# Two stage barriers of a one-core transformer trunk removed, its semaphores recycled, routing tables and gate products moved into the last output tiles

## What is computed

```python
x = x + m_lat[2] * y                                   # y: token mixer's output @ w_out
h = modulate(rmsnorm(x, norm2_w), m_lat[3], m_lat[4])
aff = softmax(h @ router_w)                            # 2048 tokens x 16 experts
gate, idx = lax.top_k(swapaxes(aff, 1, 2), 256)        # each expert takes its 256 best tokens
xs = h[idx]
hid = silu(xs @ w1[e]) * (xs @ w3[e])
y = (hid @ w2[e]) * gate
x = x + m_lat[5] * scatter_add(y, idx)
out = rmsnorm(x, final_norm_w)
```

## Time and profile before

| | us |
|---|---|
| median of 3 runs (lowest, highest) | 2226.61 (2224.59, 2227.75) |
| the profiled execution | 2225.62 |
| its span, first to last instruction | 2223.9 |
| busy: PE, DVE, ACT, POOL | 2118.4 (95%), 1372.4 (62%), 993.1 (45%), 282.8 (13%) |

### The profile page before, as it was taken

One profiled execution on the slowest core, in us unless ns is written; L12 is line 12 of the kernel. 1 busy time (PEld: TensorE's weight loads), 2 busy tenths in 40 slices (PEclk: granted clock), 3 DMA queues, 4 the chain that ended last, 5 costly groups with the idle time before them and its releaser, 6 DMA issues. The chain is left out here.

```text
span 2223.9 us, 34721 instructions
## 1 busy us (share of the span) xinstructions
PE 2118.4 (95%) x13389; PEld 1847.9 (83%) x13389; DVE 1372.4 (62%) x2077; ACT 993.1 (45%) x1619; POOL 282.8 (13%) x356
## 2 busy tenths in 40 slices
PE   6999999999999799995799999999999999999995
PEld 4778888777777588883799999999999999999993
DVE  3663648995974666746455655556555565555656
ACT  5822544344622444421444444444444444444444
POOL 0000000000001001011111122111221112211120
PEclk9999999999999899996799999999999999999997
DMA  7473333343337656328347656476565765657655
GB/s 253 147 262 105 112 92 96 122 123 94 101 121 218 230 173 199 124 108 306 129 182 254 207 199 213 180 258 207 196 213 180 261 207 190 216 180 264 207 182 225
DMA packets 188283, 407.92 MB, mean 183 GB/s; under 512 B 15956, under 2 KB 53396, under 8 KB 187300
## 3 DMA queue, kind: packets, MB, share of 16 engines
q1 hardware_dynamic: 162068, 317.84, 41.1%
q0 software_dynamic: 26128, 88.92, 12.6%
HBM read 329.59 MB, written 77.12 MB: 183 GB/s over the span
## 5 line engine op out<-in xcount | busy, mean ns | idle before, releaser
L55 PE MATMUL bh<-xt_hi,shi 128*128 128x256 f32 x2048 | 580.8, 284 | 3.2 <-DVE slo L2234 3.2
L56 PE MATMUL bh<-xt_lo,shi 128*128 128x256 f32 x2048 | 580.7, 284 | 0.0
L57 PE MATMUL bh<-xt_hi,slo 128*128 128x256 f32 x2048 | 580.6, 284 | 0.0
L2234 DVE TENSOR_TENSOR slo<-raw,shi 128x1024 fp32r<-128x1024 f32 x384 | 455.9, 1222 | 162.3 <-ACT shi L2152 157.8
L2152 ACT ACTIVATE shi<-raw 128x1024 fp32r<-128x1024 f32 x384 | 388.8, 1050 | 127.3 <-PE eby L57 127.3
L55 PEld LDWEIGHTS bh<-xt_hi,shi 128*128 128x128 f32 x2048 | 393.9, 192 | 4.3 <-issue 3.7
L56 PEld LDWEIGHTS bh<-xt_lo,shi 128*128 128x128 f32 x2048 | 393.9, 192 | 0.6
L57 PEld LDWEIGHTS bh<-xt_hi,slo 128*128 128x128 f32 x2048 | 393.8, 192 | 0.0
L55 PE MATMUL bank<-h_hi,whi 128*128 128x512 f32 x704 | 286.3, 407 | 0.0
L56 PE MATMUL bank<-h_lo,whi 128*128 128x512 f32 x704 | 278.7, 396 | 0.0
L57 PE MATMUL bank<-h_hi,wlo 128*128 128x512 f32 x704 | 278.3, 395 | 0.0
(11 more groups left out here) (336 smaller groups left out, 3145.4 us busy)
## 6 DMA issues: line engine op xcount, KB each, us to landing
raw<-in_exp_w_dram SPq DMA_DIRECT2D x96, 2048.0 KB, 11.1
uT<-stage POOLq DMA_DIRECT2D x72, 256.0 KB, 2.7
xb<-in_ada_w_dram SPq DMA_DIRECT2D x24, 512.0 KB, 5.6
wraw<-in_w_in_dram SPq DMA_DIRECT2D x22, 512.0 KB, 5.1
adaw<-in_ada_w_dram SPq DMA_DIRECT2D x8, 1024.0 KB, 10.0
xb<-in_x_dram SPq DMA_DIRECT2D x16, 512.0 KB, 4.5
xt<-in_x_dram POOLq DMA_DIRECT2D x16, 512.0 KB, 5.2
x2d<-xt POOLq DMA_DIRECT2D x16, 512.0 KB, 2.9
```

The lines of the kernel that those rows point to most:

```text
L55: nc.tensor.matmul(out, w_hi, x_hi, start=start, stop=False)
L56: nc.tensor.matmul(out, w_hi, x_lo, start=False, stop=False)
L57: return nc.tensor.matmul(out, w_lo, x_hi, start=False, stop=stop)
L2234: nc.vector.tensor_tensor(item_dst(slo, n), item_src(n), item_dst(shi, n), ALU.subtract).then_inc(S["w_lo_ready"], 1)
```

## The change

All three programs become one block. The barrier `stage_over` and both block changes go. Where a stage's buffers lie over another's, single semaphore waits take their place. Since the semaphores of projection and tail plus those of routing and experts are more than there are, Pool clears those of the projection (`recycle`) after output tile 2, when four engines have said (`left`) that they no longer use them, and the routing's and the experts' are then allocated. Tables, masks, loads, 12 of 32 gate products and the first transposes are called from within the tail's loops. In the search two gate products follow each of the rounds 0 to 9. `TD` is 7. The gather indices of expert 0 come straight from PSUM, and its first four weight items are split before its tokens.

```diff
@@ tail_stage, sync_body
+            sp.wait_ge(S["recycled"], 1)
+            sp.wait_ge(S["gated"], HEADS * NBK)
+            v.route.gate_loads(sp)            # 4 x 1 MB of ada_w, bias
+            sp.wait_ge(S["y_ready"], NQ)
+            v.route.first_expert(sp)          # 6 x 2 MB
+            sp.wait_ge(S["aff_ready"], NT)
+            v.route.weights_out(sp)           # aff to DRAM
@@ pool_body, after store(t) and x_in(t + 2)
+                if t == 2:
+                    pool.wait_ge(S["left"], 4)
+                    v.recycle()
+                    pool.sem_inc(S["recycled"], 1)
+                if t == NT - 4:
+                    pool.wait_ge(S["gated"], HEADS * NBK)
+                    v.route.masks(pool)
+                if t == NT - 3:
+                    v.route.tables(pool)
@@ tensor_body, at the end of half q
+                if q == NQ - 1:
+                    pe.wait_ge(S["recycled"], 1)
+                    pe.wait_ge(S["gated"], HEADS * NBK)
+                for _ in range({NQ - 1: 4, NQ: 1, NQ + 2: 3}.get(q, 0)):
+                    v.route.gate(pe, n_gate)
+                    n_gate += 1
@@ tensor_body, after the loop
+            pe.wait_ge(S["aff_ready"], NT // 2)
+            pe.wait_ge(S["y_read"], NQ - 2)
+            v.route.turn_weights(pe, 0)
+            for _ in range(4):
+                v.route.gate(pe, n_gate)
+                n_gate += 1
+            pe.wait_ge(S["aff_ready"], NT)
+            v.route.turn_weights(pe, 1)
@@ scalar_body
+                if q == NQ - 6:
+                    act.wait_ge(S["recycled"], 1)
+                    act.wait_ge(S["gated"], HEADS * NBK)
+                    v.route.wide_silu(act)
@@ vector_body
+                if q == NQ - 2:
+                    dve.wait_ge(S["recycled"], 1)
+                    v.route.same_masks(dve)
@@ phase_route becomes route_stage; PE's search
-    GATE_FROM, GATES = 3, 3
-    TD = 4
+    GATES = 2
+    TD = 7
-                    if GATE_FROM <= i < ROUNDS - 1:
-                        for _ in range(GATES):
+                    for _ in range(GATES if i < ROUNDS - 1 else 0):
@@ DVE's search: the masks between the rounds are gone, the copy is in halves
-                link(nc.vector.tensor_copy(afft[:, :], bthr[:, 0:2 * P]))
-                    between(i)
+                for i in range(2):
+                    dve.wait_ge(S["aff_turned"], i + 1)
+                    last = nc.vector.tensor_copy(afft[:, i * P:(i + 1) * P], (bthr, beq)[i][:, 0:P])
+                link(last)
@@ DVE, after the list
+                for s, bank in enumerate((btok, bcnt)):
+                    nc.vector.tensor_scalar(v.gidx[s][:, :], bank[:, 0:1], 0.0, None, ALU.add
+                                            ).then_inc(v.s_gather_index, 1)
@@ phase_experts, ACT (before tok_hi) and DVE (before tok_lo)
+                act.wait_ge(*v.hot_free)          # blocks_ready
+                for n in range(NR):
+                    split(0, n)
@@
+                for n in range(NR):
+                    split(0, n)
@@ trunk_kernel
-    def stage_over():
-        nc.clear_and_free_semaphores(list(in_use))
-        in_use.clear()
-        nc.all_engine_barrier()
-        stage_over()
-            phase_route(nc, v, sem)
-            phase_experts(nc, v, sem)
+                def recycle():
+                    nc.clear_and_free_semaphores(project)
+                    v.s_raw = {k: sem(f"e_raw{k[0]}{k[1]}") for k in RAW_ORDER}
+                    v.s_gather_index = sem("e_gather_index_ready")
+                    v.route = route_stage(nc, v, sem, low, high)
+                v.route.emit(block)
+            phase_experts(nc, v, sem, block, low + D * 4 + len(RAW_ORDER) * KD * 512 * 4)
```

More of the change, by code:

```diff
@@ new lines, in masks @@
+        def masks(pool):
+            pool.iota(apart[:, :], pattern=[[1, P]], base=P, channel_multiplier=-1).then_inc(S["apart_ready"], 1)
+            pool.iota(row[:, :], pattern=[[0, 1]], base=0, channel_multiplier=1).then_inc(S["row_ready"], 1)
+            pool.iota(quarter[:, :], pattern=[[1, 4]], base=0, channel_multiplier=0).then_inc(S["quarter_ready"], 1)
+            pool.wait_ge(S["quarter_ready"], 1)
+            for i in range(ROUNDS):
+                pool.tensor_scalar(steps_of[:, i, :], quarter[:, :], float(1 << (28 - 2 * i)), None, ALU.mult
+                                   ).then_inc(S["steps_made"], 1)
+            pool.memset(steps_of[:, ROUNDS, :], 0).then_inc(S["steps_made"], 1)
+            pool.memset(onesb[:, :], 1.0).then_inc(S["scan_set"], 1)
+            pool.memset(before[:, :], 1.0).then_inc(S["scan_set"], 1)
+            pool.memset(begin[:, :, :], 1.0).then_inc(S["scan_set"], 1)
+            pool.wait_ge(S["scan_set"], 3)
+            pool.memset(begin[:, :, 0:1], 0.0).then_inc(S["scan_set"], 1)
+            pool.affine_select(out=before[:, :], in_=before[:, :], compare_op=ALU.is_gt, fill=0.0, base=0,
+                               pattern=[[1, P]], channel_multiplier=-1).then_inc(S["before_ready"], 1)
@@ new lines, in turn_weights, with gate @@
+        def turn_weights(pe, i):
+            nc.tensor.transpose((bthr, beq)[i][:, 0:P],
+                                v.aff[:, 8 * i:8 * i + 8, :].rearrange("p t e -> p (t e)"), v.ident[:, :]
+                                ).then_inc(S["aff_turned"], 1)
+        def gate(pe, n):
+            i, k = divmod(n, KD)
+            if n == 0:
+                pe.wait_ge(S["silu_ready"], 1)
+            if k == 0:
+                pe.wait_ge(ada_loaded[i], 16)
+            last = nc.tensor.matmul(bgate[i // 2][:, (i % 2) * 256:(i % 2 + 1) * 256], silu_c[:, k, :],
+                                    adaw[i][:, k, :], start=(k == 0), stop=(k == KD - 1))
+            if n == 4 * KD - 1:
+                last.then_inc(S["gate_ready"], 1)
@@ L1742, in _, with emit @@
+        def emit(block):
             @block.tensor
             def _(pe):
[L1744 to L1756 removed]
@@ L2015, in loop @@
             body(NE - 1, False, True)
-        with nc.Block() as block:
+        if True:
             @block.sync
@@ L2188, in body @@
                     for f in range(FD + 1):
-                        split(e, 2 * f)
-                        split(e, 2 * f + 1)
+                        if not (first and f < NR // 2):
+                            split(e, 2 * f)
+                            split(e, 2 * f + 1)
                         if f:
```

231 lines of the change are left out of this document (126 added, 105 removed).

## The result

The changed kernel takes 2208.38 us (median of 4 runs, 2207.68 to 2208.94), the kernel before in the same comparison 2227.14 us. The ratio is 0.9918, 95% interval 0.9901 to 0.9935: 18.8 us faster, where the forecast was 3.8 and the range ended at 2218.0. The profiled execution took 2207.68 us, with a span of 2206.0.

The account below looks back on a forecast made before the run. It took the kernel as bound by the some 83 us chain between the last output product and expert 0's first product. Terms -0.1 - 2.3 - 1.4 = -3.8 us gave 2222.8 us on the median, range 2218.0 to 2226.4.

Parts of the forecast that it names:

- Parts (a) and (b): Router tail, then softmax, stage change and turning of the weights up to the first count: -0.1 us, between -0.4 and +0.3.
- The clock case: In the router tail, eight wide instructions hold the granted clock through tile 14's router product, not to the end; 50%.
- Case C: Rival for the router tail: the clock stays up to the count, -4.6 us there, -8.3 in sum, 2218.3 us; chance 12%.
- The barrier's gain is eaten by the gates that stand in its place: Before the first count: gate products on the same in-order engine use up the removed barrier's gain, leaving -0.1 us.
- The chosen case: Forecast case A: clock held through tile 14's router product only, count at about 1012.4 to 1012.9; sum -3.8 us, 50%.
- Part (c): The fifteen search rounds: 32.4 us or so against 34.65, no round over 2.3; -2.3 us (-1.6 to -2.6).
- Part (d): Ranking and one-hot tables up to the token list: seven instead of four token products on DVE cost +0.6 us.
- Part (e): Token list through gathers, turns and first splits to expert 0's first product; (d) and (e) together -1.4 us.
- The contention term: DVE splits slow Pool's gather issues: +0.7 us on the first, about +1 more on the second, taking back 0.8.
- D: Rival at expert 0's gathers: they wait for all four DVE splits, sum -1.6 us, 2225.0 us; chance 8%.
- E: Rival in the output tiles: early gate loads starve them, TensorE stalls for 11 us, 2234 us; chance 8%.
- The tables on Pool and the masks on DVE: Moved under the last output tiles, some 7 us and about 1.2 us of work, priced at zero on the path.

## Why the prediction was wrong, step by step

- **The step that failed most is one that the prediction doesn't have.** It went from "one saved elsewhere does nothing" straight to the chain after the last output product, and priced only what is there. The 32 byte tile stood in my own account of the change, and I gave it no sentence. It is 7.4 us by itself, 40% of the result. The reason was to look for time only where TensorE is not full ("TensorE is busy 95% of the span", "The gap is one stretch"): busy in the projection meant 0.233 us a product, when the output tiles of the same kernel ran products of 512 columns with other weights at 0.226, 13 steps between these two lines:

```profile
989.82 0.39 PE L56 MATMUL bank<-wo_lo,ct_hi 128*128 128x512 f32 x1
992.76 0.39 PE L57 MATMUL bank<-wo_hi,ct_lo 128*128 128x512 f32 x1
```

  That difference was in the trace of before, though nothing in it names the address.
- **Parts (a) and (b), forecast -0.1, measured -6.25.** The clock case was the wrong one. Case C, at 12%, said the clock stays up to the count, -4.6; this is what happened. The step that failed is "I expect them to hold the clock for a few microseconds more": I took the turns and router products for work under which it falls whatever stands between them. In fact the eleven microseconds with eight gates spread over them keep 1.00 until 1002 us, in all four profiled executions that have these eight gates and the aligned weights. In the one without the tile, the clock dipped between and came back (three timeline rows and a windows row):

```profile
1001.27 1.83 PE L1376 MATMUL bank<-ident,h 128*128 128x128 f32 x8
1002.89 2.41 PE L1824 MATMUL bank<-r_adaw,silu_c 128*128 128x256 f32 x6
1005.14 1.85 PE L1386 MATMUL bank<-rw,h2t 128*128 128x16 f32 x16
994.00:1007.00 13.00, 12.75 (x84) 11.43 (x83) 4.95 (x10) 4.44 (x12) 1.06 (x2) 0.87 0.86 311
```

  The turns of tile 15 took 1.83 us and the three gates 2.41, the tail 12.83. That is the fall that I forecast, behind the router product of tile 14, but not its price: the clock was back for tile 15's router product. So the stretch is near an edge, and a single execution can show either. Nor does the clock fall at one fixed point without gates. Seven profiled executions have none in the tail. In five the clock fell 3.1 to 3.5 us after the start of the last wide product, in the run with both parts moved without the staging tiles 4.4 us, and in the run with the 32 byte tile alone 6.4 us, inside tile 14's router product (2.88 us). The tail took 15.42 or 15.43 us in the five, and 15.29 and 14.26 in the other two, so of the 4.3 us a microsecond is within what executions differ by. The 4.26 us of the tail are, step by step from the rows: 0.47 up to the router product of tile 14 (its second turn takes 0.63 instead of 1.09), 1.62 in that product, 0.43 from the turns of tile 15 to the next router product, the three gates included, and 1.74 in the last one. Within C the sum was mis-sized: it has 1.6 us for the turns of tile 15, which take 0.91 until the first gate; and the count comes 2.36 us after the last router product, not 3.1 (its own terms add up to 2.7), since the gates at 2.4 GHz end only 0.65 us after softmax. The chosen case has such a slip too: its steps lead to a count at 1012.3, 0.5 us before the old one, and the sum takes 0.1.
- **"The barrier's gain is eaten by the gates that stand in its place" is false**, and its mirror is true: most of the gain is the gates'. Barrier 2.4, gates 3.9 in the tail and 0.85 in the search (the run without gates in the tail against the changed kernel).
- **Part (c) was right**: 32.39 us, forecast 32.4; no round over 2.30. That the masks and tables between the rounds were the excess is read from the rounds of both traces; no run puts them back. The 0.3 us taken off for counting products at 1.2 GHz is in part luck: rounds at the low clock are 0.01 us longer, 0.1 in all, and 0.2 lie in one round of 2.30, in which DVE waits 0.23 us behind its own step; the changed kernel and its six variants all have it, and why is open. Rounds at 1.2 GHz (1003 to 1009, 1017 to 1021) do fit two gates: 2.05 us for their four instructions at the slower pace in a 2.11 us round. That is closer than it looks, and three do not fit.
- **Part (d) was right**: +0.58, forecast +0.6, and the run with TD = 4 gives it back.
- **Part (e), forecast -2.0 from list to product, measured -3.2** (2.6 to 3.2 over the six traces with the early splits). The contention term is what was mis-sized. The first gather's issue was not slowed (1.05 us, though DVE's splits ran under all but its first 0.14), the second was (1.99, as the earlier trace rows had it), but its data were not what the second turn waited for. So the 0.8 us that I let the contention take back stayed; the first data landed 0.2 us sooner, and the first product starts 0.05 us behind the last token part instead of 0.2. The forecast's sign for this part, 13.1 us from list to product, doesn't follow from its own sum, which gives 12.5.
- **The rivals.** D, the gathers blocked for the length of all splits, is refuted for these instructions: the first gather's issue took 1.05 us and the second 1.99, not 4.6. What I took from the Trainium skill's page "SBUF — State Buffer", section "SBUF: two separate sides", for D was not what it says: there, whichever of the two starts first has the shared port pair for the whole instruction and the other blocks, so that by it a wait would end with one split and not with four. The trace agrees with that for the issues: the one that began before the splits took 1.05 us, the one that began under them took one more microsecond, with a split at 1.16 us. It doesn't show the lock itself, nor a hold in the other direction: the four splits take 4.63 us with the issues under them and without (1059.94 in the run with late splits). E did not come: the burst is there, 371 GB/s from 930 to 940 us, and PE has 10.00 of 10 us. The x rows' issue at 940.18 waited 2.15 us for a store, inside the slack, and PE has no idle time from 940 to 985 us either. The tables on Pool and the masks on DVE are free, as said: the output tiles take the same 258.4 and 258.3 us.
- **The range** left out case C's full price with the alignment on top. Without the tile the changed kernel is at 2216.04 us, 2.0 under the range by its median, though the interval of its ratio reaches into the range: the clock and the contention term alone brought it to the edge or over.

## What to carry to other kernels

Read the pace of the bounding engine's commonest instruction in every stage, not only its busy share: a stage that is 100% busy at 0.233 us where another does the like at 0.226 may have 2% to give, and an address can be the cause. Price every line of a diff, the one that seems to do nothing too. And on the path behind a dense stretch, small independent products between the short ones are not only work in the way: where they keep the granted clock at 1.00, they can give back more than they take.

## What the runs showed of the hardware

- Stationary operands of fp32r products (128x128, moving 512 columns, whi and wlo in turn) that begin 32 bytes off a multiple of 64 in SBUF run at 0.233 us a product instead of 0.228. It needs both parts at a multiple of 64; one of them gives nothing of the gain. The projection has 2112 such products, and the kernel before gains 7.4 us by it.
- The granted clock fell to 0.50 some 3 us after the last wide product in five of seven executions without gates in the tail, 4.4 and 6.4 us after it in the other two. It held at 1.00 for 11 us with eight gate products (16 instructions of 256 columns) among router products and transposes in four executions of five, and dipped to 0.57 from 1001 to 1004 us in the fifth; with five gates it fell inside the last router product.
- The clock also dips inside the projection, in which PE is 99% busy: 6 products took 0.43 us each near 629 us in the trace of before, 14 near 436 and 604 us in that of the changed kernel, each time a few microseconds behind a stretch with PE partly idle.
- A gather's issue on Pool under back-to-back two-input DVE splits took 1.99 us against 0.97 with DVE idle, but the first one, which began 0.14 us before the splits, took 1.05. The four splits took 4.63 us either way.
